# Second block of a two-block transformer in one kernel: gates by tangent inside the attentions, finer weight splits, a moved transpose, and roots on GpSimd

## The chip, the core and the metric

One core of a Trainium2 chip runs the whole kernel as a single program. The metric is the time of one execution in microseconds, the median of several; lower is better. Engines are called PE (TensorE), PEld (its weight loads), DVE (VectorE), ACT (ScalarE), POOL (GpSimd) and SP (SyncE, which starts transfers).

## The reference

Batch 1, 512 tokens, width 1024, fp32. The first block (differential and sparse attention, then an MLP) is changed only in the roots of its head norms. The second block has two layers. Both compute `h = h + (o * silu(gate)) @ w_out`:

```python
# layer A ("FOX"): 16 heads of 64, causal, with forget decays
u = rmsnorm(h); q, k, v, f, gate = split(u @ w_in_a)
q = rmsnorm(q per head); k = rmsnorm(k per head)
o = softmax(q k^T / 8 + c_q - c_k) v          # c = cumsum(log_sigmoid(f))
h = h + (o * silu(gate)) @ w_out_a
# layer B ("SWA"): 16 query heads on 4 key heads, window of 128, a sink per head
k, v = split(rmsnorm(h) @ w_kv); q, gate = split(rmsnorm(h) @ w_in_b)
o = softmax([q k^T / 8 in the band, sink]) v
h = h + (o * silu(gate)) @ w_out_b
```

## The kernel before

Raw Bass: each engine has its own instruction stream in an order written out by hand, and semaphores are the only ties between them. An engine runs its stream in order, so a wait holds everything behind it.

**Products.** Every fp32 product is three passes over a high and a low half of each operand (HI·HI, HI·LO, LO·HI). Weights come in units of 512x512, into two slots of RAW; ACT writes the high half (`split_hi`, `side_hi`), DVE the low half (`split_lo`, `side_lo`), into two slots of SPL. A run (`RUNS`) is a row of column groups; each group leaves four PSUM banks (4 x (group % 2) onwards), which ACT evicts (`evict`).

**Head norms** (`norm_one`, `norm_two`, `root`, `norm_parts`; 15 groups). ACT evicts the group. POOL squares it (L1636). DVE sums per head, scales and adds eps (L1063, L1066). ACT takes the square root (L675, in `root`, called behind each eviction). DVE takes the reciprocal (L1069), multiplies (L1072) and, for rotated groups, adds the rotated part that POOL makes (L1645, L1092, L1096).

**Late attentions** (`attend_beside`, for FOX and then SWA). Each has 8 units `m` (two heads) of 4 query tiles `i`, so 32 steps `n`; a step handles the scores of step n+1, the probabilities of n-1 and the values of n-2. Per step:
- PE: `scores_of(n+1)`, `values_of(n-2)`, `turn_p(n-1)` (transposes of probabilities, and of the q and k of a later unit, L2153 to L2157), and a quarter of a tile of the gate product (`part`, L2167).
- DVE: maxima (in SWA first the sink column, L1305; then L1308), half of the copies of transposed probabilities (L1321), reciprocals (L1315), low halves of transposed q and k (`low`, L1326).
- ACT: exponentials (L798), the other half of the copies (L806), high halves (`high`, L818), the kept output (`keep`, L829, at i = 1 of the next unit).
- POOL: scales the probabilities (L1691).

**Gates.** The gate product has 8 tiles of 128 columns from four weight units of 256 columns (`side`). All of them use one bank, `SIDE_BANK` = 3, which ACT copies out to MX (`keep_tile`, L825); PE waits for that copy before the next tile. The first `lead` tiles (1 in FOX, 2 in SWA) are made before the scores begin; the others lie in the steps of the units. The silus (L841, L875) run in the last steps. After the attention `gated_hi` (ACT, L877) and `gated` (DVE, L1361 the product with the kept output, L1356 the low half) make the left operand of the output product, tile by tile; the output product (`RUNS["fox_out"]`, `RUNS["swa_out"]`, L1739) waits for it (`y_lo`) piece by piece.

**First transposes.** Before the steps, q and k of units 0 and 1 are transposed into banks 2m + i of the half that also holds `SIDE_BANK`. In FOX these are four, and the fourth lies in bank 3; hence PE waits for its low half (`kt`) before the first gate tile. In SWA two units share a key, so there are three.

**Splits inside the attentions.** Units 2 and 3 of the gate weights and the first two of the output weights are split at i = 1 and i = 2 of every second unit (`split_at`), a half unit each time: one 128x1024 instruction, or four 128x256 ones where a norm gain is folded in (the gate weights of SWA; L594, L588 on ACT, L997, L990 on DVE).

**SP** starts the transfers in a written order: weights wait until a slot is split, decays (`decays(m)`, a row of CK per head pair) until the scores of unit m-2 are done.

## Time and profile before

| | |
|---|---|
| median of 3 runs | 1903.93 us (1900.86 to 1904.18) |
| the profiled execution: its own time | 1901.54 us |
| its span, first to last instruction | 1899.7 us |
| granted PE clock, mean (1.0 is 2.4 GHz, 0.5 is 1.2 GHz) | 0.941 |
| first block, MLP included, and the norm behind it | to 1274 us |
| FOX: input products, attention, output product | to 1423, to 1563, 1567 to 1613 us |
| norm; SWA: input products, attention, output product | to 1630, to 1699, to 1843, 1847 to 1893 us |

How to read it: the page gives busy time per engine over the whole span. Windows do the same for a stretch: where PE's busy time equals the length, PE is the bound there. The timeline shows single instructions in order of start; brackets behind a row give how long the engine was idle before it and what ended that. A unit of FOX is 15.7 us, one of SWA 12 to 22 us.

### The profile page before, as it was taken

The page shows a single profiled execution, that of the slowest core. Times are in us where ns is not written, and L with a number is a line of the kernel's source. Part 1 is how long each engine was busy: PE and PEld are TensorE (multiplying, and loading weights), DVE is VectorE, ACT ScalarE, POOL GpSimd, SP SyncE. Part 2 cuts the span into 40 slices and gives each one's busy share as a digit, 9 for nine tenths or more (in the row PEclk, how much of TensorE's full clock was granted, in tenths as well). Part 3 has the DMA queues.
Part 4 walks back from the last instruction along what each step waited for, and adds up shares of the span by engine and source line. Part 5 has one row for each costly group of instructions (what it writes and reads, how often), then busy time and mean ns, then how long its engine had stood idle before and what let it go on. Part 6 is the DMA issues. An engine that isn't in the chain of part 4 may idle for free.

```text
span 1899.7 us, 24666 instructions
## 1 busy us (share of the span) xinstructions
PE 1742.6 (92%) x9327; PEld 1354.8 (71%) x9327; DVE 894.4 (47%) x1582; ACT 718.4 (38%) x1568; POOL 367.0 (19%) x498
## 2 busy tenths in 40 slices
PE   6999788999978998998999999989998989888978
PEld 5888557868664554886888888867786767676656
DVE  3782473225445666344343244244644554455552
ACT  3322464122135666323332133133224562434451
POOL 5440242002114564011000000000102330022220
PEclk9999796999987999999999999989999999899979
DMA  6223121422102221432222322332221013220101
GB/s 174 86 92 122 50 73 56 133 89 89 45 12 56 67 58 32 155 104 96 66 90 89 110 89 96 104 111 77 87 82 45 24 36 120 67 89 24 45 23 45
DMA packets 117779, 147.64 MB, mean 78 GB/s; under 512 B 30685, under 2 KB 63733, under 8 KB 117425
## 3 DMA queue, kind: packets, MB, share of 16 engines
q1 hardware_dynamic: 116608, 145.40, 24.0%
q0 software_dynamic: 992, 0.86, 0.4%
q8 instruction: 68, 1.11, 0.2%
q14 instruction: 31, 0.25, 0.0%
q10 hardware_dynamic: 80, 0.02, 0.0%
HBM read 125.24 MB, written 4.24 MB: 68 GB/s over the span
## 4 chain that ended last, share of the span: by engine, by line
PE 81%; ACT 8%; DVE 7%; issue 3%; POOL 1%; DMA 0%; ACTq 0%; DVEq 0%; POOLq 0%
PE ps L1739 57%; PE ps L2167 4%; PE ps L1978 3%; PE ps L2002 2%; ACT pb L740 2%; PE ps L2124 2%; PE ps L2142 2%; PE ps L2087 1%; PE ps L2021 1%; PE ps L2035 1%; DVE qkt L1241 1%; DVE nm L1211 1%; ACT qkt L759 1%; PE ps L1983 1%; PE ps L1876 1%
## 5 line engine op out<-in xcount | busy, mean ns | idle before, releaser
L1739 PE MATMUL ps<-spl,ht 128*128 128x512 f32 x2496 | 584.3, 397 | 26.5 <-DVE xk L1465 8.5
L1739 PEld LDWEIGHTS ps<-spl,ht 128*128 128x128 f32 x2496 | 478.8, 192 | 129.6 <-DVE xk L1465 9.0
L1022 DVE TENSOR_TENSOR spl<-raw,spl 128x1024 fp32r<-128x1024 f32 x180 | 234.7, 1346 | 521.9 <-ACT spl L620 521.9
L620 ACT ACTIVATE spl<-raw 128x1024 fp32r<-128x1024 f32 x180 | 180.5, 1052 | 598.7 <-PE ps L1739 598.7
L1739 PE MATMUL ps<-ht,spl 128*128 128x512 f32 x1152 | 263.9, 391 | 2.0 <-DVE spl L1022 2.0
L1739 PEld LDWEIGHTS ps<-ht,spl 128*128 128x128 f32 x1152 | 217.6, 189 | 48.1 <-issue 2.9
L1739 PE MATMUL ps<-spl,uu 128*128 128x512 f32 x768 | 174.4, 389 | 0.0
L1739 PEld LDWEIGHTS ps<-spl,uu 128*128 128x128 f32 x768 | 144.2, 188 | 29.9
L1636 POOL TENSOR_TENSOR sq<-qkv 128x2048 f32<-128x2048 f32 (+1 forms) x15 | 51.5, 3436 | 372.2 <-ACT qkv L654 357.6
L2167 PE MATMUL ps<-ht,spl 128*128 128x512 f32 x384 | 108.9, 425 | 10.5 <-DVE qkt L1326 5.4
L740 ACT ACTIVATE pb<-ps,nm 128x512 f32<-128x512 f32 (+1 forms) x192 | 99.8, 530 | 45.5 <-DVE nm L1211 45.4
L1672 POOL TENSOR_TENSOR pb<-pb,rg 128x512 f32<-128x512 f32 (+3 forms) x160 | 112.8, 722 | 7.5
L1211 DVE TENSOR_REDUCE nm<-ps 128x1 f32<-128x512 f32 (+1 forms) x192 | 85.2, 485 | 54.4 <-PE ps L1983 54.2
L2167 PEld LDWEIGHTS ps<-ht,spl 128*128 128x128 f32 x384 | 72.6, 201 | 24.8 <-DVE qkt L1326 5.7
L1739 PE MATMUL ps<-ys,spl 128*128 128x512 f32 x384 | 89.2, 395 | 0.0
L1697 POOL MEMSET nws<- 128x2048 f32 x2 | 3.6, 1807 | 440.5 <-PE ps L1739 440.5
L1739 PEld LDWEIGHTS ps<-ys,spl 128*128 128x128 f32 x384 | 73.3, 191 | 15.6 <-issue 0.2
L1978 PE MATMUL ps<-qkt 64*128 64x384 f32 (+3 forms) x576 | 77.4, 377 | 7.2 <-DVE qkt L1241 3.0
L2002 PEld LDWEIGHTS ps<-idf,pb 128*128 128x128 f32 x400 | 44.9, 143 | 36.2 <-issue 29.1
L1691 POOL TENSOR_TENSOR pbf<-pbf,rr 128x512 f32<-128x512 f32 (+3 forms) x64 | 44.7, 721 | 133.6 <-DVE rr L1315 133.6
L1978 PEld LDWEIGHTS ps<-qkt 64*128 64x128 f32 x576 | 47.7, 204 | 28.2 <-issue 23.5
L1308 DVE TENSOR_REDUCE nm<-ps 128x1 f32<-128x257 f32 (+5 forms) x128 | 53.3, 437 | 30.3 <-PE ps L2104 27.7
(292 smaller groups left out, 2060.8 us busy)
## 6 DMA issues: line engine op xcount, KB each, us to landing
raw<-w_in SPq DMA_DIRECT2D x30, 1024.0 KB, 5.2
raw<-w_mlp_up SPq DMA_DIRECT2D x16, 1024.0 KB, 5.2
raw<-w_mlp_down SPq DMA_DIRECT2D x16, 1024.0 KB, 5.0
raw<-w_in_a SPq DMA_DIRECT2D x16, 1024.0 KB, 5.3
stq<-qkv SPq DMA_DIRECT2D x32, 256.0 KB, 2.7
raw<-w_in_b SPq DMA_DIRECT2D x8, 1024.0 KB, 5.4
raw<-w_proj_diff SPq DMA_DIRECT2D x4, 1024.0 KB, 5.2
stq<-qkv SPq DMA_DIRECT2D x32, 128.0 KB, 2.5
```

The lines of the kernel that those rows point to most:

```text
L620: act.activation(SPL[:, n % 2, HI, 2 * k:2 * k + 2], RAW[:, n % 2, 2 * k:2 * k + 2], ACT.Copy).then_inc(hi_done, 1)
L740: last = act.activation(p, PS[:, 2 * (idx % 2) + h, 0:w], ACT.Exp, bias=NM[:, m.slot, h, t:t + 1], accum_out=LS[:, m.slot, h, t:t + 1])
L1022: dve.tensor_tensor(SPL[:, n % 2, LO, 2 * k:2 * k + 2], RAW[:, n % 2, 2 * k:2 * k + 2], SPL[:, n % 2, HI, 2 * k:2 * k + 2].bitcast(F32), A ...
L1211: dve.tensor_reduce(top, bank[:, 0:w], AX.X, ALU.max, negate=True).then_inc(s["mx"], 1)
L1308: dve.tensor_reduce(NM[:, m % 2, h, t:t + 1], bank[:, 0:w + a.sink], AX.X, ALU.max, negate=True)\
L1636: pool.tensor_tensor(SQ[:, :, 0:w], QKV[:, :, col:col + w], QKV[:, :, col:col + w], ALU.mult)\
L1672: last = pool.tensor_tensor(p, p, RG[:, m.slot, h, t:t + 1].to_broadcast([P, w]), ALU.mult)
L1691: last = pool.tensor_tensor(p, p, RR[:, m % 2, h, t:t + 1].to_broadcast([P, w]), ALU.mult)
L1739: last = pe.matmul(PS[:, b0 + b], left[:, x], right[:, y], start=(kt == 0 and i == 0), stop=(kt == UK * g["units"] - 1 and i == 2))
L1978: pe.matmul(PS[:, 2 * (idx % 2) + h, 0:w], QKT[r, m.slot, 0, x, P * t:P * t + P], QKT[r, m.slot, 1, y, P * a.first_key(t):P * t + P], star ...
L2002: last = pe.transpose(bank[:, P * i:P * i + P], PB[:, m.slot, h, o:o + P], IDF[:])
L2167: last = pe.matmul(PS[:, turn_bank(a, SIDE_BANK)], wide(SPL[:, n % 2, x])[:, kt, cols], HT[:, y, kt], start=(kt == 0 and j == 0), stop=(kt ...
```

## The change

Computed results stay the same up to rounding. The parts:
- **Gates by tangent.** silu(g) = g (1 + tanh(g/2)) / 2. ACT no longer copies the gate bank to MX; it writes tanh(g/2) there (`tanh`), and DVE makes (tanh + 1) x bank (`gate`), which now is what frees the bank (`kept`). The silus are gone.
- **Product unit by unit.** DVE multiplies gate m by the kept output of unit m and by 0.5 at i = 2 of the next unit (`gated`). The high and low halves are made in the last unit's steps and the two steps behind (`high_in`, `gated_high`, `gated_low`); those of the last tile come after the loop. `gated_hi` and the old `gated` are gone.
- **Splits in eighths.** One 128x256 eighth per step on ACT and DVE (`split_in`, `eighth_hi`, `eighth_lo`), two per step in FOX's last unit. `hi_done` counts eighths.
- **Second keys in a score bank.** FOX's fourth transpose goes to the bank of scores 1 (`first_bank`), after the first gate tile; PE waits for its low half before scores 1. Highs and lows on ACT and DVE move with it; tanh and gate of the first tile stand ahead.
- **Roots on POOL.** (mean + eps) to the power -0.5, right behind the squares; ACT's root and DVE's reciprocal are gone.
- SP: decays 4, 6 are started ahead of the output weights that used to precede them.

Left out below: constants, semaphore lists, and the places where a half's count of 1 becomes 4.

```diff
@@ -196,10 +196,19 @@
         return m + self.lead if 0 <= m and m + self.lead < SIDE_TILES else None
-    def split_at(self, m):
-        j = m - 2 + self.lead
-        return j // 2 + 2 if j >= 0 and j % 2 == 0 and j // 2 < 4 else None
+    def split_in(self, n):
+        m, i = divmod(n, NT)
+        j, part = divmod(m - 2 + self.lead, 2)
+        if not 0 <= j < 4 or m >= self.units:
+            return []
+        if m + 1 == self.units and part == 0:
+            return [(j + 2, 2 * i), (j + 2, 2 * i + 1)]
+        return [(j + 2, NT * part + i)]
+    def high_in(self, n):
+        return {0: (0,), 1: (1,), 2: (2,), 3: (3, 4), 4: (5,), 5: (6,)}.get(n - self.steps + NT, ())
...
@@ -387,10 +396,14 @@
         PT_BANK, PV_BANK, SIDE_BANK = 0, 2, 3
+        def first_bank(a, m, i):
+            return score_bank(a, 1, 0) if m and i else turn_bank(a, 2 * m + i)
         def turned_at(a, m, i):
             if m < 2:
-                return by_tile(PS[:, turn_bank(a, 2 * m + i)])
+                return by_tile(PS[:, first_bank(a, m, i)])
             b = turn_bank(a, PT_BANK)
...
@@ -557,11 +570,12 @@
...
             decays(3)
+            decays(4)
             weights(RUNS["fox_out"], only=1)
-            decays(4)
+            decays(5)
+            decays(6)
             weights(RUNS["fox_out"], skip=1, only=1)
-            for m in range(5, FOX.units):
-                decays(m)
+            decays(7)
             sp.wait_ge(*need(FOX, "pt_tr", FOX.steps))
...
...
+                gain = LNG[:, LN_OF_UNIT[n], k:k + 1] if n in LN_OF_UNIT and n in SIDE_UNITS else 1.0
+                act.activation(wide(SPL[:, n % 2, HI])[:, k], wide(RAW[:, n % 2])[:, k], ACT.Copy, scale=gain)\
+                   .then_inc(hi_done, 1)
             def split_hi(n, hold=()):
...
@@ -667,13 +687,6 @@
...
                    .then_inc(freed["act"], 1)
-            def root(g):
-                if g["then"][0] == "norm":
-                    n, heads = g["normed"], g["then"][2]
-                    act.wait_ge(n_ms, n + 1)
-                    act.activation(RT[:, 0:NT * heads], SS[:, 0:NT * heads], ACT.Sqrt).then_inc(n_rt, 1)
             def run(groups, hold=(), primed=False, follow=False, first=None, at={}, norm=0):
...
@@ -817,41 +828,44 @@
...
                     act.activation(turned_to(m, slot, i, HI), turned_at(a, m, i), ACT.Copy).then_inc(s["th"], 1)
-                def keep_tile(k):
+                def tanh(k):
                     if k % 2:
...
                         act.wait_ge(*need(a, "tile", k // 2 + 1))
-                    act.activation(MX[:, k], PS[:, turn_bank(a, SIDE_BANK)], ACT.Copy).then_inc(s["kept"], 1)
+                    act.activation(MX[:, k], PS[:, turn_bank(a, SIDE_BANK)], ACT.Tanh, scale=0.5).then_inc(s["tanh"], 1)
                 def keep(m):
...
                        .then_inc(s["o"], 1)
-                def split(m, part):
-                    if a.split_at(m) is None:
-                        return
-                    n = g["unit"] + a.split_at(m)
-                    act.wait_ge(raw_full[n % 2], 16 * (n // 2 + 1))
-                    act.wait_ge(unit_used, n - 1)
-                    side_hi(n, part)
-                def silu(k):
-                    act.activation(MX[:, k], MX[:, k], ACT.Silu).then_inc(s["silu"], 1)
+                def split(n):
+                    for j, k in a.split_in(n):
+                        u = g["unit"] + j
+                        if k == 0:
+                            act.wait_ge(raw_full[u % 2], 16 * (u // 2 + 1))
+                            act.wait_ge(unit_used, u - 1)
+                        eighth_hi(u, k)
+                def gated_high(k):
+                    act.wait_ge(*need(a, "gated", k + 1))
+                    act.activation(HT[:, HI, k], MX[:, k], ACT.Copy).then_inc(y_hi, 1)
                 if a.is_fox:
...
                     act.wait_ge(x_parked, 16)
-                for m, i in a.first_turns():
+                for m, i in a.first_turns()[:3]:
                     high(m, i)
                 for k in range(a.lead):
-                    keep_tile(k)
+                    tanh(k)
+                for m, i in a.first_turns()[3:]:
+                    high(m, i)
                 exps(0)
...
                     if i == 0 and a.tile_at(m - 1) is not None:
-                        keep_tile(a.tile_at(m - 1))
+                        tanh(a.tile_at(m - 1))
                     if n + 1 < a.steps:
...
@@ -860,21 +874,12 @@
...
                             high(*a.turn_with(n - 1))
-                    if n >= a.steps - 1:
-                        silu(2 * (n - a.steps + 1))
-                        silu(2 * (n - a.steps + 1) + 1)
-                    if i in (1, 2):
-                        split(m, i - 1)
-            def gated_hi(a):
-                s, base = A[a.name], 2 * KT if a.is_fox else 3 * KT
-                g = SIDE[a.name]
-                act.wait_ge(unit_used, g["unit"] + g["units"])
-                for k in range(KT):
-                    if k < 2:
-                        act.activation(MX[:, 6 + k], MX[:, 6 + k], ACT.Silu).then_inc(s["silu"], 1)
-                    act.wait_ge(*need(a, "gated", k + 1))
-                    act.activation(HT[:, HI, k], MX[:, k], ACT.Copy).then_inc(y_hi, 1)
+                    split(n)
+                    if n == a.steps - NT:
+                        act.wait_ge(unit_used, g["unit"] + g["units"])
+                    for k in a.high_in(n):
+                        gated_high(k)
+                gated_high(KT - 1)
             def narrow_hi(i, n):
...
...
@@ -1001,6 +1006,15 @@
...
                 last.then_inc(lo_done, 1)
+            def eighth_lo(n, k):
+                dve.wait_ge(hi_done, 8 * n + k + 1)
+                gain = LNG[:, LN_OF_UNIT[n], k:k + 1] if n in LN_OF_UNIT and n in SIDE_UNITS else 1.0
+                last = dve.scalar_tensor_tensor(wide(SPL[:, n % 2, LO])[:, k], wide(RAW[:, n % 2])[:, k], gain,
+                                                wide(SPL[:, n % 2, HI])[:, k].bitcast(F32), ALU.mult, ALU.subtract)
+                if k % 4 == 3:
+                    last.then_inc(lo_done, 1)
             def split_lo(n):
...
...
@@ -1066,8 +1080,6 @@
...
                 dve.wait_ge(n_rt, n + 1)
-                dve.reciprocal(RT[:, 0:NT * heads], RT[:, 0:NT * heads]).then_inc(n_rs, 1)
-                dve.wait_ge(n_rs, n + 1)
                 for t in range(NT):
...
...
@@ -1326,43 +1338,49 @@
...
                                       ALU.subtract).then_inc(s["kt" if i else "qt"], 1)
-                def split(m, part):
-                    if a.split_at(m) is not None:
-                        side_lo(g["unit"] + a.split_at(m), part)
-                for m, i in a.first_turns():
+                def gate(k):
+                    dve.wait_ge(*need(a, "tanh", k + 1))
+                    dve.scalar_tensor_tensor(MX[:, k], MX[:, k], 1.0, PS[:, turn_bank(a, SIDE_BANK)], ALU.add, ALU.mult)\
+                       .then_inc(s["kept"], 1)
+                def gated(k):
+                    dve.wait_ge(*need(a, "o", k + 1))
+                    dve.wait_ge(*need(a, "kept", k + 1))
+                    dve.scalar_tensor_tensor(by_tile(MX[:, k]), kept_output(k), 0.5, by_tile(MX[:, k]), ALU.mult, ALU.mult)\
+                       .then_inc(s["gated"], 1)
+                def gated_low(k):
+                    dve.wait_ge(y_hi, (2 if a.is_fox else 3) * KT + k + 1)
+                    dve.tensor_tensor(HT[:, LO, k], MX[:, k], HT[:, HI, k].bitcast(F32), ALU.subtract).then_inc(y_lo, 1)
+                for m, i in a.first_turns()[:3]:
+                    low(m, i)
+                for k in range(a.lead):
+                    gate(k)
+                for m, i in a.first_turns()[3:]:
                     low(m, i)
...
                 norms(0)
-                for n in range(a.steps + 1):
+                for n in range(a.steps + 2):
                     m, i = divmod(n, NT)
+                    if i == 0 and a.tile_at(m - 1) is not None:
+                        gate(a.tile_at(m - 1))
                     if n + 1 < a.steps:
                         maxima(n + 1)
-                    if n >= 1:
+                    if 1 <= n <= a.steps:
                         turned(n - 1)
...
                         norms(n + 1)
-                    if n >= 1 and a.turn_with(n - 1):
+                    if 1 <= n and a.turn_with(n - 1):
                         low(*a.turn_with(n - 1))
-                    if i in (1, 2):
-                        split(m, i - 1)
-            def gated(a):
-                s, base = A[a.name], 2 * KT if a.is_fox else 3 * KT
-                def low(k):
-                    dve.wait_ge(y_hi, base + k + 1)
-                    dve.tensor_tensor(HT[:, LO, k], MX[:, k], HT[:, HI, k].bitcast(F32), ALU.subtract).then_inc(y_lo, 1)
-                for k in range(KT):
-                    dve.wait_ge(*need(a, "silu", k + 1))
-                    dve.wait_ge(*need(a, "o", k + 1))
-                    dve.tensor_tensor(by_tile(MX[:, k]), by_tile(MX[:, k]), kept_output(k), ALU.mult)\
-                       .then_inc(s["gated"], 1)
-                    if k:
-                        low(k - 1)
-                low(KT - 1)
+                    if i == 2 and m:
+                        gated(m - 1)
+                    for j, k in a.split_in(n):
+                        eighth_lo(g["unit"] + j, k)
+                    for k in a.high_in(n):
+                        gated_low(k)
+                gated(KT - 1)
+                gated_low(KT - 1)
             def narrow_lo(i, n):
...
...
@@ -1635,6 +1654,9 @@
...
                     .then_inc(n_sq, 1)
+                pool.wait_ge(n_ms, n + 1)
+                pool.tensor_tensor(RT[:, 0:NT * heads], SS[:, 0:NT * heads],
+                                   MINUS_HALF[:].to_broadcast([P, NT * heads]), ALU.pow).then_inc(n_rt, 1)
                 q = QKV[:, :, col:col + w].rearrange("p t (h d) -> p t h d", d=HD)
...
...
@@ -2080,6 +2102,8 @@
...
                     reach(pe, *need(a, "e", n - 1))
+                    if n == 1 and a.new_keys(1):
+                        pe.wait_ge(*need(a, "kt", 2))
                     w = a.width(t)
...
@@ -2146,7 +2170,7 @@
...
                     for t in range(NT):
-                        bank, col = (turn_bank(a, 2 * m + i), P * t) if m < 2 else (
+                        bank, col = (first_bank(a, m, i), P * t) if m < 2 else (
                             turn_bank(a, PT_BANK + t // 2), 256 + P * (t % 2))
...
@@ -2180,14 +2204,14 @@
...
                 pe.wait_ge(n_done, last_in[4 if a.is_fox else 1]["normed"] + 1)
-                for m, i in a.first_turns():
+                for m, i in a.first_turns()[:3]:
                     turn(m, i)
                 for k in range(a.lead):
-                    if k == 0 and a.new_keys(1):
-                        pe.wait_ge(*need(a, "kt", 2))
                     reach(pe, *need(a, "kept", k))
...
                 pe.wait_ge(freed["act"], last_in[-1]["freed"])
+                for m, i in a.first_turns()[3:]:
+                    turn(m, i)
                 pe.wait_ge(consts, 14)
...
```

## Rows read from the trace of the kernel before

**Rows 1.** The page: busy us of each engine, share of span, instructions
```profile
PE 1742.6 (92%) x9327; PEld 1354.8 (71%) x9327; DVE 894.4 (47%) x1582; ACT 718.4 (38%) x1568; POOL 367.0 (19%) x498
```

**Rows 2.** Windows: length, busy PE, PEld, DVE, ACT, POOL, clock, DMA share, GB/s
```profile
1429.00:1438.00 9.00, 9.00 (x30) 6.81 (x30) 0.00 (x0) 0.50 (x1) 0.00 (x0) 0.67 0.13 47
...
1459.06:1474.77 15.71, 15.71 (x142) 11.75 (x142) 9.74 (x21) 9.67 (x26) 5.60 (x8) 1.00 0.21 68
...
1549.85:1563.12 13.27, 9.39 (x89) 6.42 (x88) 7.27 (x17) 10.00 (x25) 3.55 (x6) 0.80 0.07 14
...
1698.87:1704.56 5.69, 5.69 (x27) 4.41 (x25) 2.08 (x6) 2.30 (x5) 3.31 (x1) 1.00 0.40 123
1704.56:1709.65 5.09, 0.01 (x2) 0.00 (x1) 4.40 (x6) 2.18 (x5) 0.29 (x1) 0.84 0.20 70
1709.65:1717.83 8.18, 8.18 (x26) 6.27 (x26) 5.69 (x7) 0.00 (x0) 1.40 (x2) 0.68 0.00 0
1717.83:1730.57 12.74, 9.89 (x101) 7.30 (x101) 6.78 (x26) 7.97 (x25) 3.61 (x7) 1.00 0.01 1
...
1743.70:1757.00 13.30, 13.30 (x123) 9.88 (x123) 6.62 (x25) 6.66 (x26) 4.31 (x8) 1.00 0.01 2
1757.00:1778.77 21.77, 18.61 (x135) 12.47 (x134) 10.38 (x34) 10.21 (x33) 4.31 (x8) 0.84 0.15 49
```

**Rows 3.** Timeline at FOX's entry: start, us, engine, line, operands, count [idle before]
```profile
1426.32 2.48 DVE L1326 TENSOR_TENSOR qkt<-ps,qkt 128x512 fp32r<-128x512 f32 x4 [1.09 <-ACT qkt L818]
...
1428.86 8.61 PE L2167 MATMUL ps<-ht,spl 128*128 128x512 f32 x24 [5.43 <-DVE qkt L1326]
```

**Rows 4.** Timeline at FOX's end
```profile
1562.43 0.69 PE L2142 MATMUL ps<-pts,qkv 128*64 128x128 f32 x4 [0.75 <-ACT pts L806]
...
1566.85 45.95 PE L1739 MATMUL ps<-spl,ht 128*128 128x512 f32 x192 [3.72 <-DVE ht L1356]
```

**Rows 5.** Timeline at SWA's entry
```profile
1714.47 0.69 DVE L1096 TENSOR_TENSOR qkv<-qkv,sq 128x512 f32<-128x512 f32 x1
1715.08 1.88 DVE L1326 TENSOR_TENSOR qkt<-ps,qkt 128x512 fp32r<-128x512 f32 x3
...
1719.34 1.28 ACT L798 ACT_TABLE_LOAD   x1 [0.89 <-DVE nm L1308]
```

**Rows 6.** Timeline of one SWA step on DVE, from its maxima to its reciprocal
```profile
1752.19 0.16 DVE L1305 TENSOR_SCALAR ps<-sink 128x1 f32<-128x1 f32 x1 [0.32 <-PE ps L2104]
...
1753.97 0.17 DVE L1315 RECIPROCAL rr<-ls 128x2 f32<-128x2 f32 x1 [0.43 <-ACT pbs L798]
```

**Rows 7.** Timeline, PE behind a split step in unit 2
```profile
1762.75 0.66 PE L2142 MATMUL ps<-pts,qkv 128*64 128x128 f32 x8 [1.15 <-ACT pts L806]
```

**Rows 8.** Groups by shape, 1426 to 1846 us: count | busy, mean ns | idle
```profile
L594 ACT ACTIVATE spl<-raw,lng 128x256 fp32r<-128x256 f32 x32 | 13.4, 502 | 7.6 <-PE ps L1739 7.6
...
L588 ACT ACTIVATE spl<-raw 128x1024 fp32r<-128x1024 f32 x8 | 8.5, 1066 | 0.0
...
L877 ACT ACTIVATE ht<-mx 128x512 fp32r<-128x512 f32 x9 | 5.6, 628 | 3.2 <-DVE mx L1361 3.2
...
L997 DVE SCALAR_TENSOR_TENSOR spl<-raw,lng,spl 128x256 fp32r<-128x256 f32 x32 | 14.2, 507 | 9.8 <-ACT spl L594 9.8
...
L990 DVE TENSOR_TENSOR spl<-raw,spl 128x1024 fp32r<-128x1024 f32 x8 | 9.8, 1227 | 9.9 <-ACT spl L588 9.9
```

**Rows 9.** Single lines: count, ns of shortest, median and longest, first and last start
```profile
L1636 POOL TENSOR_TENSOR sq<-qkv x15: 1893/3601/4451, 54.4 to 1701.2; 128x2048 f32<-128x2048 f32 x12, 128x1024 f32<-128x1024 f32 x3
...
L1667 POOL TENSOR_TENSOR rg<-rr,gt x64: 192/197/200, 580.2 to 747.4; 128x2 f32<-128x2 f32 x64
...
L675 ACT ACTIVATE rt<-ss x15: 216/230/232, 60.6 to 1707.4; 128x32 f32<-128x32 f32 x12, 128x16 f32<-128x16 f32 x3
...
L1069 DVE RECIPROCAL rt<-rt x15: 252/353/355, 60.8 to 1707.7; 128x32 f32<-128x32 f32 x12, 128x16 f32<-128x16 f32 x3
```

36 lines of the change are left out of this document (18 added, 18 removed).

## Prediction

> **What bounds the kernel now.** I read the page first: TensorE (PE) is busy for 92% of the span, so an edit on another engine is worth only what it takes out of PE's gaps [rows 1]. The change touches the second block, so next came a table of windows from 1423 us on. There a window whose PE busy time equals its length has nothing to give to the other engines, and a window with less does. In the steady units of the first of the two late attentions (FOX) PE is busy for 15.71 of 15.71 us. Units of the second (SWA) without split work are full too, 13.30 of 13.30 us [rows 2]. The gaps lie in four places: the entry to FOX, the last unit of each attention, the entry to SWA, and the SWA units that split weights. The timeline of each gap then gives what ended it.
>
> **FOX entry: about -7.5 us.** Before, PE's first gate product waits until VectorE (DVE) has split all four first transposes, 5.43 us idle, because the fourth transpose lies in the bank of the gates. It then runs 8.61 us for 24 matmuls, and that stretch has a granted clock of 0.67 [rows 2, 3]. After, the fourth transpose goes to a score bank after the product, so the product follows the third transpose at once. With no pause ahead of it I take the 5.69 us that the same 24 matmuls last at a clock of 1.00 [rows 2]. That is 5.43 + 2.92 = 8.35. Against it: the gate (one DVE pass over a 128x512 bank) and the low half of the fourth transpose (0.69) now stand before the first maxima, and the second scores wait for that low half. The transposed bank used to be ready. I charge 0.8. Bounds 5.4 (the product stays slow) to 8.4.
>
> **SWA entry: about +7.9 us, the price of the change.** `lead` is 2 here: two gate products come before the scores, and the second needs the bank back. Before, ScalarE (ACT) copied the bank out, and PE idled 5.09 us, then ran the second product in 8.18 us, while DVE was still busy with the norm of the last query columns [rows 2]. After, the bank is freed by the DVE gate. DVE runs in order, and ahead of the gate stand the whole norm of that group, up to 1715.16, and three low halves, up to 1716.96 [rows 5]. Gate at 1717.65, product 8.18, scores at 1725.8 instead of 1717.8: +8.0. That ACT no longer stands in its root wait doesn't help, since tanh isn't the last to come. Two corrections. The exp table load of 1.28 us stood in the first softmax step [rows 5], and tanh now takes a load earlier, in idle time; the gate of the second product stands before the first maxima in its place: -0.7. And the root: it cost 0.23 of square root, a reciprocal of 0.35 and two hand-offs, some 0.7 in all [rows 9]; on GpSimd no row shows a power. The nearest, a multiply of two elements a partition, takes 0.19 [rows 9]; 32 elements of the plain multiply would be about 0.25. The far end is 3.6, what a multiply of 2048 takes [rows 9]. I take 1.2, nearer to the small ones, as only 32 elements are raised: +0.5, bounds -0.4 to +3.0. The other 14 roots lie beside PE work; a late root of the first query columns would delay the entry by its excess, within that bound. Rotation work on GpSimd waited for the norm already.
>
> What a page says on this: the Trainium skill (ScalarE: Activation LUTs, Rules for kernel authors) has ScalarE as the only option for a square root, and (GPSIMD Engine Reference, Engine selection) GpSimd as about half as fast in two-input elementwise work. Those rules would leave the root where it was. Even at twice the DVE's 0.35 for the reciprocal, an estimate from the second page, the root would be 0.7 and the sum unchanged within 0.5.
>
> **The steady units.** Three things are added to each unit: a gate (about 0.7 on DVE, reading PSUM), the product with the output (0.69, on DVE) and four eighths of a split, one per step, at 0.50 on ACT and 0.51 on DVE [rows 8], in place of halves every second unit. The copy of the gates becomes a tanh of the same size, and the silus go.
> FOX: a step has 3.93 us of PE work. DVE is held from its maxima to the end of the exponentials, longer than in SWA as the tiles are up to twice as wide, but the step is longer too, so an addition of 0.5 to 1.2 about fills it. I charge 0.15 to 0.2 for each of six units: +1.0, bounds 0 to +4.
> SWA: a PE step with gate work is 3.3 us (13.30 / 4). DVE is held for 1.95 of it (1752.19 to 1754.14) [rows 6]. An eighth fits into the rest; with a gate or the output product a step comes out up to 0.8 late, and PE has about 1.2 in hand, as it needs the copies only after the next scores. What goes is the old split: four of them in a row take 1.7 on ACT, then 1.7 on DVE, and PE stands 1.15 to 1.4 us in each of four steps of units 0 and 2 (one of the four is shown [rows 7]), some 5.2; about 1.2 more in unit 4 and behind late low halves. In unit 2 the stalls are followed by a clock of 0.84 over 21.77 us [rows 2]: about 7.0 us at 1.2 GHz, in which 3.5 are lost. 5.2 + 1.2 + 3.5, less 0.7 of new stalls: -9.2, bounds -3 to -11.
>
> **The two ends: about -0.6 and +0.7.** It looks as if 3.73 us went at each end: PE's last product of the attention ends, and the output product starts 3.72 later, behind silu, product, high and low half [rows 4]. But seven high (0.63) and low halves (0.69) now stand inside the last unit and the two steps after it, and there PE isn't the bound (in FOX 9.39 busy of 13.27 us [rows 2]; SWA's last unit is alike): DVE and ACT hand each other the work. Each of three steps before the last scores grows by a high and then a low, 1.3: +3.9. Before the last copies the table load and two silus (2.4) give way to an eighth and two highs with their lows (1.7 to 2.4): -0.8. FOX: 3.9 - 0.8 - 3.7 = -0.6. In SWA the eighths of the last two units, 8 x 1.0, replace two pairs of 1.07 + 1.23 [rows 8]: +3.5, some 2.2 of it in slack: +0.7. Bounds -4 to +3 each. The order of the queues on SyncE changes by one place only: decay loads wait for scores that are done before the weights that follow them are due.
>
> **Sum.** -7.5 + 1.0 - 0.6 + 7.9 - 9.2 + 0.7 = -7.7 us. The profiled execution took 1901.5 us (span 1899.7), so it would take 1893.8. It is 2.4 below the median of the three runs, and from that median the same sum gives 1896.2; I say 1896.
>
> **Rivals.**
> A, as above: 1896, own range 1890 to 1900. Chance 0.50.
> B, the moved halves are hidden: DVE and ACT find room in the last units and the 3.7 at each end is won. For it: PE idles in the last unit and runs slowly, so some of the growth is already paid. Against it: DVE and ACT alternate there without pause. -7.7 - 7.3 = -15: 1889. Chance 0.17.
> C, no gain in the SWA units: an eighth needs ACT and then DVE, so each step holds DVE for 1.95 + 0.4 + 0.5 + 0.5 = 3.35, as long as PE's 3.3, and the eight stalls become thirty-two small ones: SWA units -3, FOX units +3, total +0.5: 1904. For it: the step sum. Against it: PE's 1.2 in hand, once per step. Chance 0.17.
> D, slower: the same place, DVE's queue in SWA, but a step of over 3.3 us on average makes DVE the bound of all units: with gate, product and low halves spread evenly a step is 1.95 + 1.4 + 0.35 + 0.35 = 4.05, at worst 0.75 over PE's over 20 steps, +15 in place of -9; half of that is likelier, +8 in all: 1912. It decides as soon as DVE's sum per step passes PE's. Chance 0.12.
> E, tanh isn't in the table that exp uses: each gate brings two loads of 1.28 [rows 5], 2.6 us on ACT in 14 units, of which about 1 is hidden: +22: 1918. Chance 0.04. By the Trainium skill (ScalarE: Activation LUTs, Table sets: the hidden batching unit) exp and tanh are in one set, and a switch costs about 2.66 us with its drain. By that rule E is out; no row shows a tanh.
>
> **How the numbers follow.** The range takes in B and C and the unknown root: 1886 to 1907. About 0.2% (3.8 us) is what a measurement of this kernel can tell from no change. Faster by more: nearly all of A, B, a little of C: 0.68. Same: the rest of A, most of C: 0.19. Slower: D, E: 0.13.
>
> **What would show it.** Right: no idle before PE's first gate product in FOX, and its 24 matmuls in under 6.5 us; PE idle for about 13 us before the second product of SWA, ended by the DVE gate, and scores about 8 us later after the first product than before; SWA units with PE stalls under 0.5 us each and a clock of 1.00; the last unit of FOX about 3 us longer, and the output product starting at once. Wrong: a table load beside a tanh; a power of over 2 us; DVE busy without gaps in SWA while PE waits.

## The result, and where the time went

The changed kernel takes 1920.22 us (median of 4 runs, 1919.64 to 1923.05), the kernel before 1902.39 on the same chip (1899.95 to 1904.18): ratio 1.0101, 95% interval 1.0089 to 1.0113. It is slower by 1%, and the forecast was 0.3% faster. The profiled execution has a span of 1917.8 us against 1899.7, and a granted clock of 0.938 against 0.941.

The page after, in the parts that answer to [rows 1] and [rows 9]. The groups read: line, engine, operation, out<-in, shapes, count, busy us, mean ns, idle time before them and what ended it:

```profile
PE 1749.6 (91%) x9327; PEld 1358.1 (71%) x9327; DVE 918.6 (48%) x1619; ACT 705.5 (37%) x1569; POOL 453.5 (24%) x514
PE ps L1761 50%; PE ps L2191 3%; PE ps L2000 3%; POOL rt L1658 2%; PE ps L2024 2%; ACT pb L751 2%; POOL sq L1667 2%; PE ps L2148 2%; PE ps L2166 1%; POOL sq L1655 1%; PE ps L2043 1%; PE ps L2111 1%; PE ps L2057 1%; DVE nm L1223 1%; DVE qkt L1253 1%
L1658 POOL TENSOR_TENSOR rt<-ss,minus_half 128x32 f32<-128x32 f32 (+1 forms) x15 | 73.7, 4916 | 58.1 <-DVE ss L1080 58.1
L1084 DVE TENSOR_TENSOR qkv<-qkv,rt 128x512 f32<-128x512 f32 (+1 forms) x60 | 34.3, 633 | 75.4 <-POOL rt L1658 75.4
```

The 15 powers (L1658) take 4.9 us each on average, and DVE's multiply by the root (L1084) stands 75.4 us for them. PE is busy 7 us more, and the power is on the chain that ended last. Then PE's waits after (engine, line, waited for: us in total, times, longest):

```profile
PE ps L1761 <- DVE spl L1036: 19.7, 8, 5.0
...
PE ps L2191 <- DVE mx L1343: 11.3, 1, 11.3
```

The first row is new in size: it was 5.9 us in 2 waits before. The input products wait for DVE's low halves of weights. To place it, take the starts and ends of PE's rows in both timelines and subtract stage by stage. All stages together give the 18.1 us by which the spans differ:

| stage | before | after | difference | forecast |
|---|---|---|---|---|
| start to the last input product of FOX | 1421.7 | 1442.3 | +20.6 | 0 |
| FOX: last input product to first scores | 15.7 | 7.2 | -8.5 | -7.5 |
| FOX: first scores to those of the last unit's third tile | 112.5 | 116.2 | +3.8 | +1.0 |
| FOX: from there to the output product | 17.0 | 17.65 | +0.65 | -0.6 |
| output product, norm, input products of SWA | 129.0 | 129.6 | +0.6 | 0 |
| SWA: last input product to first scores | 21.9 | 36.1 | +14.2 | +7.9 |
| SWA: units 0 to 5 | 94.8 | 84.1 | -10.7 | -9.2 |
| SWA: units 6 and 7, to the output product | 34.3 | 32.2 | -2.1 | +0.7 |
| SWA: output product | 45.9 | 45.5 | -0.4 | 0 |

Apart from the entry to SWA, which is 6.3 us dearer than forecast, the second block behaves nearly as forecast. The larger part of the loss is in a stage where the forecast looked at no row: 19.5 of the 20.6 us are in the first run of input products, 177.2 us long before and 196.7 after. Three windows of it, first before, then after (busy us of each engine with its count, granted clock, DMA share, GB/s):

```profile
60.00:80.00 20.00, 20.00 (x90) 16.57 (x89) 17.23 (x13) 6.09 (x9) 11.13 (x3) 1.00 0.17 54
80.00:100.00 20.00, 20.00 (x90) 16.57 (x89) 17.22 (x14) 6.09 (x9) 8.59 (x3) 1.00 0.33 106
120.00:140.00 20.00, 20.00 (x90) 16.54 (x90) 17.26 (x13) 6.08 (x9) 11.14 (x3) 1.00 0.24 71
```

```profile
60.00:80.00 20.00, 19.54 (x87) 15.88 (x86) 11.99 (x10) 5.00 (x8) 12.13 (x3) 1.00 0.17 54
80.00:100.00 20.00, 14.72 (x60) 11.54 (x59) 14.43 (x11) 5.96 (x8) 13.22 (x4) 0.94 0.17 54
120.00:140.00 20.00, 15.03 (x56) 11.90 (x55) 15.19 (x10) 3.98 (x7) 12.52 (x4) 0.83 0.16 53
```

Before, PE is full, and DVE (third busy value) is busy for 17.2 of 20 us. Full on PE doesn't mean room on DVE. One normed group of that run in DVE's timeline, before and then after, and in the third fence PE's row of after (start, length, engine, line, operation; in brackets the idle time ahead and what ended it):

```profile
80.80 2.27 DVE L1063 TENSOR_REDUCE ss<-sq 128x32 f32<-128x2048 f32 x1
83.10 0.18 DVE L1066 TENSOR_SCALAR ss<-ss 128x32 f32<-128x32 f32 x1
83.58 0.35 DVE L1069 RECIPROCAL rt<-rt 128x32 f32<-128x32 f32 x1 [0.30 <-ACT rt L675]
83.97 2.50 DVE L1072 TENSOR_TENSOR qkv<-qkv,rt 128x512 f32<-128x512 f32 x4
86.39 4.57 DVE L1022 TENSOR_TENSOR spl<-raw,spl 128x1024 fp32r<-128x1024 f32 x2
93.34 2.29 DVE L1092 TENSOR_TENSOR qkv<-qkv,ct 128x2048 f32<-128x2048 f32 x1 [2.38 <-POOL sq L1645]
```

```profile
86.05 2.27 DVE L1077 TENSOR_REDUCE ss<-sq 128x32 f32<-128x2048 f32 x1
88.36 0.18 DVE L1080 TENSOR_SCALAR ss<-ss 128x32 f32<-128x32 f32 x1
94.07 2.50 DVE L1084 TENSOR_TENSOR qkv<-qkv,rt 128x512 f32<-128x512 f32 x4 [5.54 <-POOL rt L1658]
96.49 4.53 DVE L1036 TENSOR_TENSOR spl<-raw,spl 128x1024 fp32r<-128x1024 f32 x2
```

```profile
97.85 2.47 PE L1761 MATMUL ps<-spl,ht 128*128 128x512 f32 x5 [5.03 <-DVE spl L1036]
```

The sum comes every 22.8 us before (58.03, 80.80), every 27.6 after (58.41, 86.05): 4.9 more, for a wait of 5.54 in place of 0.30 and a reciprocal. The low halves behind the multiply come that much later, and PE stands 5.03 us for them. Of a group's 22.8 us DVE stood still for only 2.7 before (0.30 + 2.38), so there was nothing to take it from. Each group takes DVE's queue 4.9 us longer, and its fourth multiply starts at 149.95 us instead of 130.28.

That is also why most of the other roots cost nothing here. One normed group of FOX's input products, before:

```profile
1338.60:1360.40 21.80, 21.80 (x98) 18.06 (x97) 12.36 (x15) 6.24 (x10) 3.60 (x1) 1.00 0.30 97
```

PE is as full as in the first run, but DVE is busy for only 12.4 of 21.8 us: no head is rotated there, and two low halves take 2.35 us together, not 4.57. After, PE has no idle in the same stretch (21.55 of 21.55 us) with a power in it.

The entry to SWA, PE after (before: [rows 2, 5]):

```profile
1717.22 1.09 PE L2177 MATMUL ps<-idf,qkv 128*128 128x128 f32 x4 [4.28 <-DVE qkv L1108]
1722.75 7.01 PE L2191 MATMUL ps<-ht,spl 128*128 128x512 f32 x24
1741.07 8.07 PE L2191 MATMUL ps<-ht,spl 128*128 128x512 f32 x24 [11.31 <-DVE mx L1343]
1749.07 0.62 PE L2111 MATMUL ps<-qkt 64*128 64x256 f32 x6
```

The wait for the gate is there as forecast (11.31 us, where the forecast said about 13; before 5.09 for the copy), and ahead of it a second wait, of 4.28, for the norm of the first query columns, which a power has made late.

### The profile page after: what moved, and what is told of

It is laid out like the page before. It is cut to its first block, busy times and chain, and to the rows that moved or that the text cites. A ratio compares the mean times of both kernels' runs of the same rounds, so it can differ in the third digit from the quotient of the medians.

```text
span 1917.8 us, 24718 instructions
## 1 busy us (share of the span) xinstructions
PE 1749.6 (91%) x9327; PEld 1358.1 (71%) x9327; DVE 918.6 (48%) x1619; ACT 705.5 (37%) x1569; POOL 453.5 (24%) x514
## 4 chain that ended last, share of the span: by engine, by line
PE 72%; DVE 10%; ACT 8%; POOL 5%; issue 4%; DMA 0%; ACTq 0%; DVEq 0%; POOLq 0%
PE ps L1761 50%; PE ps L2191 3%; PE ps L2000 3%; POOL rt L1658 2%; PE ps L2024 2%; ACT pb L751 2%; POOL sq L1667 2%; PE ps L2148 2%; PE ps L2166 1%; POOL sq L1655 1%; PE ps L2043 1%; PE ps L2111 1%; PE ps L2057 1%; DVE nm L1223 1%; DVE qkt L1253 1%
## 5 line engine op out<-in xcount | busy, mean ns | idle before, releaser
L640 ACT ACTIVATE spl<-raw 128x1024 fp32r<-128x1024 f32 x180 | 180.4, 1051 | 716.8 <-PE ps L1761 716.8
L1658 POOL TENSOR_TENSOR rt<-ss,minus_half 128x32 f32<-128x32 f32 (+1 forms) x15 | 73.7, 4916 | 58.1 <-DVE ss L1080 58.1
L1713 POOL TENSOR_TENSOR pbf<-pbf,rr 128x512 f32<-128x512 f32 (+3 forms) x64 | 48.9, 786 | 118.0 <-DVE rr L1327 118.0
L1084 DVE TENSOR_TENSOR qkv<-qkv,rt 128x512 f32<-128x512 f32 (+1 forms) x60 | 34.3, 633 | 75.4 <-POOL rt L1658 75.4
```

The lines of the kernel that those rows point to most:

```text
L640: act.activation(SPL[:, n % 2, HI, 2 * k:2 * k + 2], RAW[:, n % 2, 2 * k:2 * k + 2], ACT.Copy).then_inc(hi_done, 4)
L1658: pool.tensor_tensor(RT[:, 0:NT * heads], SS[:, 0:NT * heads], MINUS_HALF[:].to_broadcast([P, NT * heads]), ALU.pow).then_inc(n_rt, 1)
L1713: last = pool.tensor_tensor(p, p, RR[:, m % 2, h, t:t + 1].to_broadcast([P, w]), ALU.mult)
```

## The experiments

Theory 1: the power on POOL costs far more than the 1.2 us charged, and DVE stands in order behind it; the rest of the change is worth some -9. Rival: other edits share the loss. The kernel before is timed beside each group of runs, at 1901.6, 1901.5, 1901.4 and 1900.3 us in the four. One caution on single executions: up to the last input product of FOX, kernels that run the same work there lay between 1419.0 and 1422.7 us, so a sum over one profile is good to some 3 us.

**Roots back.** The changed kernel with the old roots.

```diff
-                pool.tensor_tensor(RT[:, 0:NT * heads], SS[:, 0:NT * heads],
-                                   MINUS_HALF[:].to_broadcast([P, NT * heads]), ALU.pow).then_inc(n_rt, 1)
...
+                    act.activation(RT[:, 0:NT * heads], SS[:, 0:NT * heads], ACT.Sqrt).then_inc(n_rt, 1)
...
+                dve.reciprocal(RT[:, 0:NT * heads], RT[:, 0:NT * heads]).then_inc(n_rs, 1)
```

> The changed kernel with the roots alone put back (square root on ScalarE, reciprocal on VectorE). Theory 1, the power on GpSimd holds VectorE's queue: the first block and the FOX input products lose their 20.6 us again, and the entry to SWA its late norms, some 6 us (the norm of the first query columns ends when it did before, and the gate that frees the bank comes 6 us earlier): 1920.2 - 20.6 - 6.1 = 1893.5 us. TensorE then has no idle in the first run of products (177.2 us long, as before). Theory 2, the loss came from the other edits too (the finer splits change the semaphore counts and so the order in the first run): 1905 us or more, with part of the idle in the first run left.

Measured: 1890.82 us, ratio to the kernel before 0.9950 (0.9933 to 0.9966). The first run is 175.9 us long with no idle, and the entry to SWA 29.5 instead of 36.1. PE's wait for the gate is 13.01 us, as forecast. Theory 1 holds. With the old roots the rest of the change is a gain of 0.5%.

**The power alone, in the kernel before.** The reverse edit.

> The kernel before with the roots alone moved to GpSimd. Theory 1: +20.6 us in the first block and the FOX input products, and at the entry to SWA about 5.4 (the scores then wait for VectorE's low halves instead of the second gate product): 1902.4 + 26 = 1928 us, so that the rest of the change is worth about -8. Theory 2, the power is dear only together with the rest of the change: under 1915 us.

Measured: 1926.16 us, ratio 1.0135 (1.0118 to 1.0152). First run 196.4 us, entry to SWA 27.15 instead of 21.9. So the power costs 24.6 us alone, and 29.4 (1920.2 - 1890.8) with the rest of the change. Of the 4.8 us between the two, the entry to SWA holds 1.4 (6.7 against 5.2), where the gate stands behind the late norm; the first run differs by 1.6, and no more of it is settled, as single profiles differ by some 3 us.

**What a power costs.** Scratch powers at the start of the kernel with the roots back.

```diff
+            for o, w in ((128, 1), (129, 8), (137, 16), (153, 32), (185, 128)):
+                pool.tensor_tensor(PW[:, o:o + w], PW[:, 0:w], MH[:].to_broadcast([P, w]), ALU.pow)
+            for o, w in ((313, 32),):
+                pool.tensor_tensor(PW[:, o:o + w], PW[:, 0:w], MH[:].to_broadcast([P, w]), ALU.mult)
```

> As roots_back, with five powers on GpSimd at the start, on scratch data, of 1, 8, 16, 32 and 128 elements a partition, and one multiply of 32. From the two sizes in the changed kernel (2.90 us for 16, 5.42 for 32) a line: 0.38 + 0.158 per element. If the cost is per element and belongs to the power itself: 0.5, 1.6, 2.9, 5.4 and 20.6 us, and the multiply of 32 under 0.3. Rival, the time was the wait for data or a start-up of the first power (code being loaded): the later ones are far shorter than the first.

The groups of these lines, by shape:

```profile
L1611 POOL TENSOR_TENSOR pw_t<-pw_t,mh 128x128 f32<-128x128 f32 x1 | 20.7, 20713 | 0.0
L1611 POOL TENSOR_TENSOR pw_t<-pw_t,mh 128x32 f32<-128x32 f32 x1 | 5.4, 5406 | 0.0
L1611 POOL TENSOR_TENSOR pw_t<-pw_t,mh 128x16 f32<-128x16 f32 x1 | 2.9, 2887 | 0.0
L1611 POOL TENSOR_TENSOR pw_t<-pw_t,mh 128x8 f32<-128x8 f32 x1 | 1.6, 1647 | 0.0
L1611 POOL TENSOR_TENSOR pw_t<-pw_t,mh 128x1 f32<-128x1 f32 x1 | 0.6, 577 | 0.1
L1613 POOL TENSOR_TENSOR pw_t<-pw_t,mh 128x32 f32<-128x32 f32 x1 | 0.2, 231 | 0.0
```

The price is the operation's own, 0.16 us per element of a partition, on top of some 0.4. The multiply of 32 is 23 times cheaper than the power of 32. The time of this kernel (1925.6, one run) says nothing more: the 31 us of scratch work delay what POOL does behind them, and PE's first instruction, which waits for a constant that POOL writes, starts at 35.08 us instead of 8.10.

**Does it have to be waited for?** The power stays on POOL, and DVE writes low halves of weights between the sum and the multiply, and between the multiply and the rotated part.

`norm_one(g, 0)` is its part up to the mean, `norm_one(g, 1)` the multiply by the root.

```diff
-                        norm_one(groups[k - 1])
+                        norm_one(groups[k - 1], 0)
                     for u in range(g["units"]):
                         if g["unit"] + u + 2 < end:
                             split_lo(g["unit"] + u + 2)
                         if k and u == 0:
+                            norm_one(groups[k - 1], 1)
+                        if k and u == 1:
                             norm_two(groups[k - 1])
```

> The changed kernel with the power left on GpSimd; in the runs of products VectorE writes the low halves of the next weight unit between the sum and the multiply by the root, and those of the second unit before the rotated part is added. Theory 1, it is not the power's 5.4 us that costs but the place of the wait in VectorE's queue: work of 4.6 us covers it, the first run of products is back to 177 us, and the time is 1920.2 - 19.5 = 1900.7 us; the entry to SWA keeps its loss. Rival, the longer chain through GpSimd (square, power, rotation) is the bound of each group whatever VectorE does in between: over 1912 us.

Measured: 1911.78 us, ratio 1.0050 (1.0033 to 1.0067): between the two, and nearly at the rival's 1912. DVE's timeline, and in the second fence POOL's:

```profile
84.38 2.29 DVE L1078 TENSOR_REDUCE ss<-sq 128x32 f32<-128x2048 f32 x1 [3.78 <-POOL sq L1662]
86.79 2.40 DVE L1036 TENSOR_TENSOR spl<-raw,spl 128x1024 fp32r<-128x1024 f32 x2
93.33 2.50 DVE L1087 TENSOR_TENSOR qkv<-qkv,rt 128x512 f32<-128x512 f32 x4 [4.14 <-POOL rt L1665]
```

```profile
86.96 6.33 POOL L1665 TENSOR_TENSOR rt<-ss,minus_half 128x32 f32<-128x32 f32 x1 [2.61 <-DVE ss L1081]
95.90 6.69 POOL L1674 TENSOR_TENSOR sq<-qkv,st 128x1024 f32<-128x1024 f32 x2 [2.61 <-DVE qkv L1087]
```

The low halves cover only 2.40 us, as they are quick when POOL isn't rotating, and the sums still come every 27.1 us (84.38, 111.45). Square, sum, power, multiply, rotation and addition of one group are a chain between POOL and DVE, and the next square waits for its end. In this order PE stands only 5.7 us in the run instead of 13.9, because splits go first, but the chain of 27 us is over PE's 22.8. The first run is 184.6 us long. So of its loss of 19.5 us 12 were the place in the queue, and 7.4 stay with the length of the chain. This order also delays one of the input products of FOX by 2.4 us, behind the decay sums.

**Near the price that was assumed.** The power on 5 of the elements, a multiply by a constant for the others, so most head norms have no root.

```diff
-                pool.tensor_tensor(RT[:, 0:NT * heads], SS[:, 0:NT * heads],
-                                   MINUS_HALF[:].to_broadcast([P, NT * heads]), ALU.pow).then_inc(n_rt, 1)
+                pool.tensor_tensor(RT[:, 0:5], SS[:, 0:5], MINUS_HALF[:].to_broadcast([P, 5]), ALU.pow)
+                pool.tensor_tensor(RT[:, 5:NT * heads], SS[:, 5:NT * heads],
+                                   ONES[:, 0:1].to_broadcast([P, NT * heads - 5]), ALU.mult).then_inc(n_rt, 1)
```

> The changed kernel with the power on GpSimd for the first 5 of the 32 (or 16) elements only; the rest are copied by a multiply with a constant, so most head norms have no root (the output is not the reference's). By the sizes measured (0.58 us for one element, 1.65 for 8) the power takes 1.17 us and the copy 0.23: 1.4 in all, about the 1.2 of the prediction. If its price alone was wrong, the time is that of roots_back plus one or two tenths per late group: 1891 to 1894 us, and the first run of products has no idle. Rival: VectorE has no room in that run even for 1 us (it stands only 2.4 + 0.3 us in a group of 22.8): 1896 us or more, with idle in the first run.

Measured: 1896.15 us, ratio 0.9976 (0.9962 to 0.9990). The power takes 1.17 us and the copy of the other elements 0.23, so this root is 1.4 us, not 1.2. The rival holds: the root still costs about 5 us against the kernel with the roots back (the ratios are 0.9976 and 0.9950, and their intervals just overlap). The first run is 180.4 us long, not 177.2 or 175.9, and the entry to SWA 0.5 longer. PE has idle in the first run again:

```profile
113.70 6.60 PE L1762 MATMUL ps<-spl,ht 128*128 128x512 f32 x28 [0.81 <-DVE spl L1036]
137.24 3.01 PE L1762 MATMUL ps<-spl,ht 128*128 128x512 f32 x12 [0.98 <-DVE spl L1036]
```

**The second early gate tile of SWA in another bank.** On top of the roots back.

```diff
+        def side_bank(a, k):
+            return score_bank(a, 1, 0) if a.is_swa and k == 1 else turn_bank(a, SIDE_BANK)
...
-                    reach(pe, *need(a, "kept", k))
+                    if k:
+                        pe.wait_ge(freed["act"], last_in[-1]["freed"])
                     side(k, 0, KT)
...
+                    if n == 1 and a.is_swa:
+                        pe.wait_ge(*need(a, "kept", 2))
```

> As roots_back, and the second early gate tile of SWA goes to the first score bank of step 1, so that no gate has to free a bank before it. If the loss at the entry to SWA is the wait for VectorE's gate, the second product follows the first at once, the scores start when VectorE has written the low halves, 8 us earlier than in roots_back: 1885.5 us. Rival: the scores wait for VectorE in any case and the scores of step 1 now wait for two gates there: at most 3 us gained, 1890.5 us or more.

Measured: 1884.32 us, ratio 0.9912 (0.9896 to 0.9929). Entry to SWA 20.8 us instead of 29.5 (1.0 is given back in unit 0). The wait for the bank was the price of DVE's gate, and another bank avoids it.

**The fourth transpose back** in the bank of the gates, on the kernel with the roots back.

```diff
-            return score_bank(a, 1, 0) if m and i else turn_bank(a, 2 * m + i)
+            return turn_bank(a, 2 * m + i)
...
+                    if k == 0 and a.new_keys(1):
+                        pe.wait_ge(*need(a, "kt", 2))
```

> As roots_back, with the fourth first transpose of FOX back in the bank of the gates, before the gate product. By the ledger's own bound the entry to FOX loses what it gained: the 24 matmuls of the first product wait some 5 us again and run at the lower clock, first scores 8.5 us later after the last input product than in roots_back (15.7 instead of 7.15 us). Rival: the gate by tangent is what changed the entry, and less than 6 us come back.

Measured (one run, 1896.39): entry to FOX 15.68 us, not 7.17. That is 8.5 us for the transpose alone. Behind the first scores 0.8 of it comes back: unit 0 is 0.15 shorter, and the last part is 17.00 us, not 17.65, as PE is busy for 10.73 us with the same matmuls and not for 11.40, at a granted clock of 0.73 instead of 0.67.

**The splits in their old places.** Roots back, four 128x256 pieces in a row; in a second kernel DVE also waits for all four high pieces before it starts, as before.

```diff
-        if not 0 <= j < 4 or m >= self.units:
+        if not 0 <= j < 4 or m >= self.units or part or i not in (1, 2):
             return []
-        if m + 1 == self.units and part == 0:
-            return [(j + 2, 2 * i), (j + 2, 2 * i + 1)]
-        return [(j + 2, NT * part + i)]
+        return [(j + 2, 4 * (i - 1) + k) for k in range(4)]
```

and in the second kernel also

```diff
-                dve.wait_ge(hi_done, 8 * n + k + 1)
+                dve.wait_ge(hi_done, 8 * n + 4 * (k // 4) + 4)
```

> As roots_back, with the same 128x256 split instructions given four in a row at two steps of every second unit (the old places), not one per step. If the places are what gained, the SWA units 1, 3 and 5 show their stalls and the low clock again: SWA from first scores to the output product some 10 us longer than in roots_back, FOX 0 to 3 us shorter or longer. Rival: the silus that left the last steps and the gates were the gain: under 4 us in SWA.

> As halves_back, but VectorE waits for four high pieces before it writes its first low one, as in the kernel before. If the finer hand-over, not the place of the splits, took away most of SWA's stalls, units 0 to 5 of SWA go from 87.1 us (halves_back) to about 94 (before: 94.8). Rival: the tangent, which took the silus and the copies out of ScalarE's queue, did it: they stay under 89.

Measured (one run each): 1886.24 and 1897.58 us. (The kernel before had one 128x1024 instruction in place of four pieces where no gain is folded in, in FOX and for the output weights.)

| | before | roots back | old places, piece by piece | old places, all four first |
|---|---|---|---|---|
| FOX, first scores to output product | 129.5 | 133.9 | 128.1 | 132.3 |
| SWA, units 0 to 5 | 94.8 | 84.15 | 87.1 | 93.6 |

Two surprises. In SWA the place is worth 3 us and the finer hand-over from ACT to DVE 6.5. In FOX the new places lose 5.75, of which 3.5 up to the scores of the last unit's third tile (116.2 against 112.75) and 2.3 behind them (17.65 against 15.4). Why is in DVE's groups of the low pieces of 128x256 in FOX, one per step (roots back), then four in a row:

```profile
L1022 DVE SCALAR_TENSOR_TENSOR spl<-raw,spl 128x256 fp32r<-128x256 f32 x32 | 23.1, 733 | 8.8 <-ACT spl L617 8.8
L1020 DVE SCALAR_TENSOR_TENSOR spl<-raw,spl 128x256 fp32r<-128x256 f32 x32 | 14.3, 505 | 3.2 <-ACT spl L615 3.2
```

The same 32 instructions take 733 ns instead of 505, and DVE waits 5.6 us longer for ACT. One per step, they fall into the time in which POOL scales the probabilities (roots back):

```profile
1458.04 2.04 POOL L1721 TENSOR_TENSOR pbf<-pbf,rr 128x512 f32<-128x512 f32 x2 [3.12 <-DVE rr L1338]
1459.17 1.20 DVE L1022 SCALAR_TENSOR_TENSOR spl<-raw,spl 128x256 fp32r<-128x256 f32 x1
```

Piece by piece, those that run with no POOL instruction beside them take 0.41 to 0.43 us (3 of 32 one per step, 20 of 32 in a row), the others 0.43 to 1.20. That POOL is what slows them is read off these rows; no run tried it by itself.

**The gate behind the maxima**, on the kernel with the other bank.

```diff
-                    if i == 0 and a.tile_at(m - 1) is not None:
-                        gate(a.tile_at(m - 1))
                     if n + 1 < a.steps:
                         maxima(n + 1)
+                    if i == 0 and a.tile_at(m - 1) is not None:
+                        gate(a.tile_at(m - 1))
```

> As roots_bank, with VectorE's gate behind the maxima of its step, not before them. In units 2 to 6 of FOX TensorE stands 0.46 us each for the low half of a transposed key and takes 0.73 us more a unit than before. If the gate ahead of the maxima makes ScalarE's chain late, the unit is back at 15.71 us: 3.5 us in all. Rival: the product with the output or the eighths, slowed by GpSimd's work beside them, make it late: no change of the unit (16.44 us).

Measured (one run, 1886.28): refuted, and the rival's "no change" isn't met either, as it got worse. FOX units go from 16.44 to 16.80 us and SWA's units 2 and 4 from 13.3 to 14.4. The gate wasn't what made the low half of the key late.

**Only one half inside the last unit**, on the former.

```diff
-        return {0: (0,), 1: (1,), 2: (2,), 3: (3, 4), 4: (5,), 5: (6,)}.get(n - self.steps + NT, ())
+        return (0,) if n == self.steps - NT + 1 else ()
```

> As gate_late, with only the first high and low half of the output product's left operand inside the last unit, and the other seven behind it, beside the output product, which takes them one by one. If those halves on ScalarE and VectorE are what bounds the last unit, each end is 3 to 5 us shorter (FOX from the scores at step 30 to the output product: 17.65 us in the changed kernel, 13 to 14.5 here; SWA alike) and the output products keep their 46 us. Rival: the output product stalls for the halves behind it and gives the gain back (output products 48 us or more).

Measured (one run, 1886.18): FOX's last part 15.35 us against 16.75, SWA's units 6 and 7 30.9 against 31.8, output products unchanged (46.2, 45.3). The mechanism holds, at 1.4 and 0.85 us instead of 3 to 5: most of the halves' work fills gaps that were there. The time as a whole doesn't show it (1886.18 against 1886.28), as this profile is 2.9 us longer up to the last input product of FOX.

**The parts together**: roots back, the other bank, FOX's splits in the old places piece by piece, SWA's one per step, one half inside the last units, the gate ahead of the maxima.

> As roots_bank (roots back, second early gate tile of SWA in a score bank), with FOX's splits in the old places (four pieces at two steps of every second unit), SWA's one per step, and only the first high and low half of the output product's operand inside the last units. If the parts add up: 1884.3 - 5.75 (FOX, halves_back against roots_back) - 1.4 - 0.85 (the ends, ends_late against gate_late) = 1876.3 us. Rival: the two edits of FOX's end share one gain: 1878 to 1879.

Measured: 1875.38 us (1874.67 to 1880.35), ratio 0.9872 (0.9846 to 0.9898). It is faster than both kernels, 1.3% under the one before and 2.3% under the changed one, and the parts add up within 1 us.

## Why the prediction was wrong

**The step that failed** is the root. It took 1.2 us for the power, with a far end of 3.6 from a multiply of 2048 elements, and it said that the other 14 roots lie beside PE work, and so cost nothing. The price was wrong for all of them, and "beside PE work" for the four of the first run.
- The price is 5.42 us, and 2.90 in the three groups of 16 elements. The rows it was bounded by [rows 9] are of other operations, and an operation that no row shows isn't bounded by how many elements it touches: a power of 32 costs more than a multiply of 2048.
- "Beside PE work" was read off PE's column. In the first run DVE was nearly as full as PE, and its queue holds the low halves that PE needs next. Even near the assumed price, at 1.4 us, the root costs about 5 us (1896.15 against 1890.82), not 0.5.
The bound of the forecast, -0.4 to +3.0, was put on one root at one place; the change had 15. At 4.9 us for each of four groups the loss of the first run is nearly the product, 19.5. The prediction's own sign of being wrong, a power of over 2 us, is there in all 15.

That the kernel with the power of five elements lands on 1896.15, where the forecast was 1896.0, is chance: the kernel before ran at 1900.3 beside it, so it gains 4.2 us and not the 7.7 of the sum.

**FOX entry**, -7.5: -8.5 (with the fourth transpose back in its old bank the whole of it is lost again). The 24 matmuls take 5.74 us at a clock of 1.00:

```profile
1443.35 5.74 PE L2191 MATMUL ps<-ht,spl 128*128 128x512 f32 x24
```

The 0.8 charged for the delay behind it was too much; unit 0 is 0.15 us longer.

**FOX steady**, +1.0 with bounds 0 to +4: +3.8. The mechanism was the one named (DVE's step fills), the term was mis-sized: an eighth was priced at 0.51, from rows of a burst, and one per step takes 0.73 there. Units 2 to 6 take 16.44 instead of 15.71.

**FOX end**, -0.6: +0.65. **SWA end**, +0.7: -2.1. Both lie within their bounds, but neither has the sign of the forecast. The 3.9 us charged for the halves were too much (moving all but one out of the last unit gives back 1.4 in FOX and 0.85 in SWA). In FOX the new places of the eighths, two per step there, cost about 2.3 (17.65 against 15.4 with four in a row), which the sum left out.

**SWA entry**, +7.9 of which 0.5 for the root: without the power it is +7.5 (29.46 - 21.92), so the queue ahead of DVE's gate was read rightly. The power added 6.7, not 0.5, and went past the bound of +3.0 that was given for it.

**SWA steady**, -9.2: -10.7. Units 1, 3 and 5, counted from one unit's first scores to the next (the forecast counts them as 0, 2 and 4), are 15.6 us each, and unit 3 has its clock back (1.00; [rows 2] have 0.84):

```profile
1788.65:1804.27 15.62, 15.62 (x135) 11.07 (x135) 10.38 (x33) 8.99 (x29) 5.11 (x9) 1.00 0.00 1
```

The reading that ACT's four pieces and then DVE's four make PE wait was right; the larger part of the gain is that DVE now follows ACT piece by piece, which the forecast didn't separate from the new places.

**Sum without the root**: -8.2 forecast, -9.4 by the stages of the profile, -10.7 by the medians of roots_back and its own kernel before (1890.82 - 1901.56).

**Rivals.** None of them named the root. D, slower by DVE's queue, put the right engine at the wrong place: in the steady units of SWA DVE never became the bound (10.4 busy of 15.6 us). C and E are out: the SWA units gained, and one table load stands at a tanh. The rule of the Trainium skill that was weighed, ScalarE for the square root (ScalarE: Activation LUTs, Rules for kernel authors), would have left the root where the runs show that it belongs. ScalarE isn't the only option, as GpSimd's power gave the roots here too, but at 5.42 us for 32 elements against 0.23 for the square root and 0.35 for the reciprocal. The rule was set aside with a sum "unchanged within 0.5"; the runs say 24.6 us (in the kernel before) to 29.4 for going against it. A rule that speaks against an edit deserved a rival of its own, with the 15 roots counted.

## What to carry to other kernels

An operation that no row shows has no price yet: multiply the doubt by how often it is issued, and read a window of every stage in which it stands, not only of those with gaps. A full PE says nothing of the room on the engine that feeds it; look at that engine's busy time and the idle of one period. When work is cut finer for two engines, the finer hand-over may be worth more than the new places, and spreading it can cost where a third engine works in between.

## What the runs showed of the hardware

- GpSimd's power is about 0.16 us per element of a partition (577, 1647, 2887, 5406, 20713 ns for 1, 8, 16, 32, 128), a multiply of 32 elements 231 ns.
- DVE's 128x1024 low halves take 2.29 us each while POOL rotates (4.57 for two) and 1.20 beside a power (2.40 for two). The power in turn goes from 5.42 to 6.33 us with them beside it. So of GpSimd's instructions here the rotation slows DVE and the power doesn't.
- After PE's waits of 5 us in the first run the granted clock of the 20 us windows fell to 0.94 and 0.83, from 1.00. The run's 768 matmuls take 182.7 us in place of 177.2; with 13.9 us of idle that makes the 19.5 by which it grew.
